# Rotary embedding: the swap of rotated channels by small DMAs and GpSimd in place of permutation matmuls

## The reference

```
h = rms_norm(x, norm_g)
qa, ka, va, za, qb, kb, vb, zb, ga, gb = split(h @ w_in)
qa = partial_rope(qa); ka = partial_rope(ka)       # branch A only; 8 query heads, 2 key heads of 64
ya = swa_sink_attention(qa, ka, va) * silu(za)     # keys: own chunk of 64 and the one before
yb = chunked_relpos_attention(qb, kb, vb) * silu(zb)
merged = sigmoid(ga + bias_a) * (ya @ w_br_a) + sigmoid(gb + bias_b) * (yb @ w_br_b)
out = rms_norm(x + merged @ w_out, final_g)

def partial_rope(t):            # per head: channels 0-7 are x1, 8-15 are x2, 16-63 stay
    return concat(x1 * cos - x2 * sin, x2 * cos + x1 * sin, rest)
```

## Time and profile before

| | us |
|---|---|
| median of 3 runs (lowest to highest) | 3417.24 (3415.64 to 3418.3) |
| the profiled execution, its own time | 3415.78 |
| its span, first to last instruction | 3414.0 |
| PE busy | 3342.3 (98%) |
| DVE, ACT, POOL busy | 1488.9, 1422.8, 1306.6 (44%, 42%, 38%) |

### The profile page before, as it was taken

How to read it: one execution, slowest core, us unless ns; L and a number is a source line. 1 busy time by engine, 2 the same in 40 slices (tenths; PEclk the granted TensorE clock), 3 DMA queues, 4 the chain that set the end, 5 groups by cost and what they waited for, 6 DMA issues and landing times.

```text
span 3414.0 us, 48305 instructions
## 1 busy us (share of the span) xinstructions
PE 3342.3 (98%) x16328; PEld 2498.0 (73%) x16328; DVE 1488.9 (44%) x3097; ACT 1422.8 (42%) x2969; POOL 1306.6 (38%) x1087
## 2 busy tenths in 40 slices
PE   8999999999999999999999999999999999999998
PEld 6667876678766787667876678766787667876676
DVE  4662355513555135551355513555135551355512
ACT  4443444434444344443444434444344443444432
POOL 3334442345423454234542344423454234542244
PEclk9999999999999999999999999999999999999999
DMA  4222431224311242112421124311242112521123
GB/s 156 62 62 87 172 99 50 62 87 167 99 50 62 87 168 99 50 62 87 168 99 52 61 86 168 98 56 61 83 172 94 55 60 84 173 93 56 56 82 116
DMA packets 97782, 319.53 MB, mean 94 GB/s; under 512 B 9984, under 2 KB 26624, under 8 KB 95360
## 3 DMA queue, kind: packets, MB, share of 16 engines
q1 hardware_dynamic: 97536, 316.34, 28.4%
HBM read 299.52 MB, written 16.78 MB: 93 GB/s over the span
## 4 chain that ended last, share of the span: by engine, by line
PE 85%; issue 6%; DVE 5%; POOL 2%; ACT 1%; DMA 0%; DVEq 0%; POOLq 0%; SPq 0%; ACTq 0%
PE acc L909 16%; PE acc L911 14%; PE acc L910 14%; PE ps_o L1004 6%; PE ps_pt L973 5%; PE sc L953 4%; PE sc L909 3%; PE sc L910 3%; PE sc L911 3%; POOL w_lo L755 2%; PE sc L944 2%; PE sc L851 2%; PE sc L852 2%; PE sc L853 2%; PE sc L876 1%
## 5 line engine op out<-in xcount | busy, mean ns | idle before, releaser
L755 POOL TENSOR_TENSOR w_lo<-w_raw,w_hi 128x512 fp32r<-128x512 f32 x928 | 1209.2, 1309 | 2060.0 <-ACT w_hi L1058 2059.3
L909 PE MATMUL acc<-h_hi,w_hi 128*128 128x512 f32 x2432 | 1010.4, 415 | 2.4 <-DVE q L1316 2.4
L911 PE MATMUL acc<-h_hi,w_lo 128*128 128x512 f32 x2432 | 952.7, 392 | 0.0
L910 PE MATMUL acc<-h_lo,w_hi 128*128 128x512 f32 x2432 | 950.4, 391 | 0.0
L1058 ACT ACTIVATE w_hi<-w_raw 128x512 fp32r<-128x512 f32 x928 | 574.2, 624 | 392.9 <-DMA w_raw<-w 116.5
L909 PEld LDWEIGHTS acc<-h_hi,w_hi 128*128 128x128 f32 x2432 | 456.3, 188 | 212.3 <-issue 133.9
L911 PEld LDWEIGHTS acc<-h_hi,w_lo 128*128 128x128 f32 x2432 | 456.4, 188 | 101.5
L910 PEld LDWEIGHTS acc<-h_lo,w_hi 128*128 128x128 f32 x2432 | 458.1, 188 | 75.7
L1146 ACT ACTIVATE probs_b<-sc,negm 128x640 f32<-128x640 f32 x256 | 203.2, 794 | 373.6 <-DVE negm L1263 373.0
L1153 ACT ACTIVATE probs_t<-ps_pt 128x512 f32<-128x512 f32 (+1 forms) x272 | 150.7, 554 | 264.8 <-PE ps_pt L973 264.8
L1288 DVE SCALAR_TENSOR_TENSOR part<-th,sc 128x512 f32<-128x512 f32 x64 | 43.9, 686 | 468.0 <-PE sc L911 467.8
(11 more groups left out here) (140 smaller groups left out, 3923.8 us busy)
## 6 DMA issues: line engine op xcount, KB each, us to landing
w_raw<-w SPq DMA_DIRECT2D x464, 512.0 KB, 3.5
rows<-x SPq DMA_DIRECT2D x36, 512.0 KB, 7.4
xt<-x_t SPq DMA_DIRECT2D x16, 1024.0 KB, 10.0
out<-rows SPq DMA_DIRECT2D x32, 512.0 KB, 2.8
x_in<-x SPq DMA_DIRECT2D x28, 512.0 KB, 5.4
cs<-rope_tab SPq DMA_DIRECT2D x8, 512.0 KB, 4.3
bias<-near SPq DMA_DIRECT2D x1, 1024.0 KB, 13.3
g_out<-final_g SPq DMA_DIRECT2D x1, 512.0 KB, 11.5
```

The lines of the kernel that those rows point to most:

```text
L755: pool.tensor_tensor(w_lo[n % 2][:, c], w_raw[n % 2][:, c], w_hi[n % 2][:, c].bitcast(FP32), ALU.subtract).then_inc(w_split, 1)
L909: pe.matmul(dst[:, :], hi, src_hi[:, k, :], start=begin, stop=False)
L910: pe.matmul(dst[:, :], hi, src_lo[:, k, :], start=False, stop=False)
L911: mm = pe.matmul(dst[:, :], lo, src_hi[:, k, :], start=False, stop=end)
```

## The change

The permutation matmuls, `pre_hi`, `pre_lo` and four DVE operations go. ACT makes only `pre`, in one of two buffers in turn. SP then waits until ACT has emptied the bank and issues four DMAs from SBUF to SBUF, each of 8 channels by 512 tokens, which put the swapped channels into `rot` (also two buffers, zero in the channels that do not turn; the second one shares its place with other data and is set to zero anew in each block). POOL multiplies `pre` by the cosines into the destination (step `rope_in`), and in step `rope` waits for the four DMAs, multiplies `rot` by the signed sines and adds. `rope` of `q1` to `q3` stands one quarter later in the list, and the four score tiles of head pair 0 and their exponentials stand two quarters later.

```diff
-        at_ = QUARTERS * O_TILES + 14 + t
+        at_ = QUARTERS * O_TILES + 16 + t
         lead[at_] = [("scores", 0, t), *lead[at_], ("exps", 0, t)]
...
-            fill[at_ + 2] = [("rope", s), *fill[at_ + 2]]
+            fill[at_ + 3] = [("rope", s), *fill[at_ + 3]]
...
-USES_ACC = ("job", "turn_v", "rope_k", "rope", "norm")
+USES_ACC = ("job", "turn_v", "norm")
...
+            def swap(b, step):
+                i = ROPE_NO[("rope_k" if step[1] == "k" else "rope", step[2])] % 2
+                wait_freed(sp, b, step)
+                for h0 in (0, HD):
+                    for to, src in ((h0, h0 + HALF_ROT), (h0 + HALF_ROT, h0)):
+                        sp.dma_start(rot[i][to:to + HALF_ROT, :], pre[i][src:src + HALF_ROT, :]).then_inc(rope_swapped[i], 16)
...
                     if step[0] == "mm" and step[2] == 0 and not (last and step[1] + 2 >= NW):
                         load_w(b, step[1] + 2)
+                    elif step[0] == "job" and step[1] in ("k", "q") and step[2] < PAIRS:
+                        swap(b, step)
...
+                    if step == ("mm", TILES.index(("k", 0)), 0):
+                        hold(h_done, (b + 1) * KT)
+                        pool.memset(rot[1][:, :], 0.0).then_inc(rot_zeroed, 1)
...
+                        pool.tensor_tensor(roped(step), pre[no % 2][:, :], cs[:, 0, :], ALU.mult).then_inc(rope_cos, 1)
+                    elif step[0] in ("rope", "rope_k"):
+                        no = ROPE_NO[step]
+                        hold(rope_cos, b * NROPE + (no + 1))
+                        pool.wait_ge(rope_swapped[no % 2], b * (64 * (3 - no % 2)) + 64 * (no // 2 + 1))
+                        pool.tensor_tensor(rot[no % 2][:, :], rot[no % 2][:, :], cs[:, 1, :], ALU.mult).then_inc(rope_sin, 1)
+                        pool.wait_ge(rope_sin, b * NROPE + (no + 1))
+                        pool.tensor_tensor(roped(step), roped(step), rot[no % 2][:, :], ALU.add).then_inc(rope_done, 1)
...
-                    elif kind in ("rope", "rope_k"):
-                        claim(b, step)
-                        pe.wait_ge(rope_lo, b * NROPE + (ROPE_NO[step] + 1))
-                        pe.matmul(bank(step)[:, :], perm_r[:, :], pre_hi[:, :], start=True, stop=False)
-                        pe.matmul(bank(step)[:, :], perm_r[:, :], pre_lo[:, :], start=False,
-                                  stop=True).then_inc(acc_full, 1)
...
-                    if not (first and no == 0):
-                        act.wait_ge(rope_done, b * NROPE + no)
-                    act.activation(pre[:, :], ps, ACT.Copy,
+                    if not first or no >= 2:
+                        act.wait_ge(rope_done, b * NROPE + max(no - 1, 0))
+                    if no == 1:
+                        act.wait_ge(rot_zeroed, b + 1)
+                    act.activation(pre[no % 2][:, :], ps, ACT.Copy,
                                    scale=SCALE if name == "q" else 1.0).then_inc(free(step), 1)
-                    wait_freed(act, b, step)
-                    act.activation(pre_hi[:, :], pre[:, :], ACT.Copy).then_inc(rope_hi, 1)
```

More of the change, by code:

```diff
@@ L31 @@
 HD = 64
+HALF_ROT = HD // 8
 PAIRS = 4
@@ L360, with program @@
 check_ring()
-def program(nc, x, x_t, w, near, far, sinks, norm_g, final_g, gate_b, rope_tab, perm, eye, out):
+def program(nc, x, x_t, w, near, far, sinks, norm_g, final_g, gate_b, rope_tab, eye, out):
     off = [(nc.sbuf_base + 63) // 64 * 64]
@@ L408, in program @@
     y_lo_at = y_at + 4 * SETS * BLK
-    pre = at("pre", [P, BLK], FP32, y_lo_at + 4 * BLK * 3)
-    pre_lo = at("pre_lo", [P, BLK], FP32R, y_lo_at + 4 * BLK * 6)
-    pre_hi = at("pre_hi", [P, BLK], FP32R, y_lo_at + 4 * BLK * 7)
+    pre = [at(f"pre{i}", [P, BLK], FP32, y_lo_at + 4 * BLK * n) for i, n in enumerate((3, 6))]
     bias = sb("bias", [P, 9, A_KEYS])
@@ L427, in program @@
     ident = sb("ident", [P, P])
-    perm_raw = sb("perm_raw", [P, P])
-    perm_r = sb("perm_r", [P, P], FP32R)
+    rot = [sb("rot0", [P, BLK]), at("rot1", [P, BLK], FP32, y_lo_at + 4 * BLK * 7)]
     far_sb = sb("far_sb", [P, 8])
@@ L487, in program @@
     pair_valued = sem("pair_valued")
-    rope_hi = sem("rope_hi")
-    rope_lo = sem("rope_lo")
+    rope_swapped = [sem(f"rope_swapped{i}") for i in range(2)]
     rope_cos = sem("rope_cos")
+    rope_sin = sem("rope_sin")
+    rot_zeroed = sem("rot_zeroed")
     rope_done = sem("rope_done")
@@ L519, in program @@
     c_dve = sem("c_dve")
-    N_CONSTS = 6
+    N_CONSTS = 5
     ADDED = HALVES * TT - O_BANKED
@@ L685, in _ @@
             load_w(0, 1)
-            for dst, src in ((perm_raw[:, :], perm), (g_out[:, :], final_g), (bias[:, 0:8, :], near), (far_sb[:, :], far),
+            for dst, src in ((g_out[:, :], final_g), (bias[:, 0:8, :], near), (far_sb[:, :], far),
                              (sink_sb[:, :], sinks), (gb_raw[:, :], gate_b)):
@@ L689, in _ @@
             sp.dma_start(cs[:, :, :], rope_tab[0]).then_inc(cs_in, 16)
+            sp.wait_ge(zeroed, 6)
             def body(b, first, last):
@@ L731, in _ @@
             pool.memset(v_b[:, 0:TT, :], 0.0).then_inc(zeroed, 1)
-            pool.wait_ge(zeroed, 5)
+            pool.memset(rot[0][:, :], 0.0).then_inc(zeroed, 1)
+            pool.wait_ge(zeroed, 6)
             def rsqrt(which, t, n, got, got_count, mid, done, count):
@@ L756, in split_lo, with roped @@
                                    ALU.subtract).then_inc(w_split, 1)
+            def roped(step):
+                return k_a[:, P:P + BLK] if step[0].endswith("_k") else q[POS[step[1]] % 2][:, :]
             rsqrt_x(0)
@@ L782, in body @@
                             pool.tensor_copy(v_b[:, 0:TT, c:c + P], v_b[:, TT:2 * TT, c:c + P]).then_inc(kept, 1)
+                    elif step[0] in ("rope_in", "rope_in_k"):
+                        job_ = ("job", "k" if step[0] == "rope_in_k" else "q", step[1])
+                        bank_, k = WHERE[job_]
+                        hold(acc_free[bank_], b * ON_BANK[bank_] + (k + 1))
+                        if step[0] == "rope_in_k" and not first:
+                            hold(kept, (b - 1) * NKEEP + (KEEP_NO[("keep_k", PAIRS - 1)] + 1))
+                        pool.wait_ge(cs_in, 16 * (b + 1))
+                        no = ROPE_NO[(step[0].replace("_in", ""), step[1])]
+                        pool.tensor_tensor(roped(step), pre[no % 2][:, :], cs[:, 0, :], ALU.mult).then_inc(rope_cos, 1)
[6 more added lines that the diff above has]
+                        pool.tensor_tensor(roped(step), roped(step), rot[no % 2][:, :], ALU.add).then_inc(rope_done, 1)
                     elif step[0] == "next_rstd" and not last:
@@ L826, in _ @@
             turn_rstd(0)
-            pe.wait_ge(zeroed, 5)
+            pe.wait_ge(zeroed, 6)
             def token_products(b, n, c):
@@ L1300, in body @@
                         job_done(b, first, step)
[L1301 to L1319, removed]
                     elif kind == "scores":
@@ L1408, in rope_tables @@
     tab[0] = 1.0
-    perm = np.zeros((P, P), np.float32)
     for h0 in (0, HD):
         for i in range(half):
-            for c in (h0 + i, h0 + half + i):
+            for c, sign in ((h0 + i, -1.0), (h0 + half + i, 1.0)):
                 tab[0, c] = np.cos(ang[:, i])
-                tab[1, c] = np.sin(ang[:, i])
-            perm[h0 + half + i, h0 + i] = -1.0
-            perm[h0 + i, h0 + half + i] = 1.0
+                tab[1, c] = sign * np.sin(ang[:, i])
     tab = tab.reshape(2, P, NBLK, BLK).transpose(2, 1, 0, 3)
-    return np.ascontiguousarray(tab), perm
+    return np.ascontiguousarray(tab)
 def kernel(x, norm_g, w_in, a_sinks, b_rel_bias, w_br_a, w_br_b, gate_bias, w_out, final_g):
@@ L1462 @@
     far = np.ascontiguousarray(np.broadcast_to(b_rel_bias[0][:, 2 * P], (P, 8)))
-    rope_tab, perm = rope_tables()
+    rope_tab = rope_tables()
     arrays = {
@@ L1470 @@
         "gate_b": np.ascontiguousarray(gate_bias[0].reshape(2 * KT, P).T),
[L1471 removed]
+        "rope_tab": rope_tab, "eye": np.eye(P, dtype=np.float32),
     }
```

6 lines of the change are left out of this document (2 added, 4 removed).

## The result

The changed kernel takes 3427.28 us (median of 6 runs, 3422.96 to 3431.79), the kernel before 3416.33 (6 runs, 3415.22 to 3418.3): the ratio is 1.0033, 95% [1.002, 1.0045]. It is slower by some 11 us, where 12.7 us less was forecast, and it lies just outside the range. The profiled execution took 3425.59 us, its span 3423.8.

What follows compares the result with a forecast made beforehand. PE, busy 98% of the span, was taken as the bound. Per block -2.87 - 1.15 + 1.58 + 0.85 = -1.59 us, times 8 is -12.7: 3403.1, with 1.5 for the median 3404.6, rounded 3405; range 3383 to 3426.

Steps and rivals of the forecast that it cites:

- step 5: Loads of tiles 7 and 8 wait behind swap issues on SP, so `turn_v` starts 1.58 us later per block (+0.8 to +5.9).
- rival C: Both loads land after 5.4 us in place of 3.6 behind the small DMAs: 29 us more, 3434; chance 0.05.
- Rival B: PE's 3.2 us wait at `turn_v` drops the clock, eight times 2.5 us on top of the forecast: 3425; chance 0.13.
- points 2 and 3: Per block, removed matmuls of `q1` to `q3` save 2.87 us; PE's waits for DVE's and ACT's rotary work save 1.15.
- point 6: Scores of the first pair two quarters later: PE waits 0.85 us per block for ACT's copy of the first transposes.
- Points 1 and 5: Removed matmuls of `k0` and `q0` save 0.94 us per block, a gain counted inside the later loads' 1.58 us cost.
- rival A: Full gain: the loads do not decide, `turn_v` keeps its 0.69 us wait, -4.11 us per block, 3384; chance 0.17.
- Points 7 and 8: POOL's 15 new operations per block cost nothing; DVE operations meeting POOL taken as nothing, 7.4 us kept for the range.

Runs made afterwards that it cites:

- e3: The changed kernel with 18 matmuls that nobody reads added per block ahead of `turn_v`, to fill PE's wait: 3413.18 us, ratio 0.9988.
- e10: The changed kernel with two swap DMAs in place of four per rotary, the second head of each pair not swapped: 3396.54 us, ratio 0.9944.
- e7: The changed kernel with the swap of `k0` alone issued behind the next tile's load, the query swaps still ahead of theirs: 3399.67 us, ratio 0.9944.
- e1: The changed kernel with SP issuing every swap behind the next tile's load and not ahead of it: 3376.28 us, ratio 0.9878.
- e4a: The kernel before with only the four score tiles of pair 0 and their exponentials two quarters later: 3419.66 us, ratio 1.0011.
- e11: e1 with the four score tiles of pair 0 back at their old place, two quarters earlier: 3371.05 us, ratio 0.9867.
- e8: e1 with POOL making the cosine product of each rotary twice, 40 operations more: 3378.9 us, ratio 0.989.

## Why the prediction was wrong

Two steps failed: step 5, "the loads behind the swaps", put the four issues at 1.80 us where they took 2.82, and the sum put the fall of the clock at nothing, where it cost 16.5 us. It took both to turn the sign. By the sum at the end of this section the kernel would be 4.6 us faster than before without the fall, and e3, which has the late loads without the fall, is 4.4 us faster (3413.18 against 3417.59).

**Step 5, the term that was mis-sized.** The chain was the right one, and all its parts but one agree within 0.1 us: the landing (3.6 and 0.10 forecast, 3.62 together), copy to issue (0.65, 0.62), split to copy (0.53, 0.54). The four issues were taken from loads issued in pairs, 0.45 each, 1.80 us. They took 2.82 us to the load, 0.70 each. Twice 1.02 is 2.04, of which the other parts, slightly shorter, give back 0.2: the chain from copy to `turned` was 15.18 long and not 13.36, and `turn_v` came 3.38 later and not 1.58. In eight blocks that is 14.4 us. The landing of 3.6 also answers rival C, which had 5.4. e10 confirms it: the mean wait goes from 40.1 / 8 = 5.01 to 18.9 / 8 = 2.36, 2.65 less, where two turns save 2 x (2.82 - 1.48) = 2.68. The bounds (0.8 to 5.9) held this, but they were made by a landing of 5.4; the issue was given no more than 0.54, because the rows at hand were all of loads over 128 partitions. The step named the four issues as its weak place, rightly, and the range did not draw on it far enough.

**Rival B came true on top.** With 3.2 us of waiting it had 0.13. The waits were 4.8 to 5.2, and the clock fell in all eight blocks. The price was put at 2.5 us each from the start of the kernel; it is 1.4 to 2.8, 16.5 in all, and e3 shows 14.1 of it by filling the wait. The Trainium skill, "TensorE: Matmul & The Clock Gate", section "What's actually happening", which takes the throttled state as the default and activity as its release, goes with e3: same lateness, PE active, clock at 1.00. Even at the forecast 3.2 us the fall was probably the likelier outcome: no run has a wait of that length, but at 2.2 to 2.9 us, in e7 and e10, it came in 11 of 16 blocks. Against the fall the prediction had only the longest wait seen without one, 1.6 us, which, as it says itself, tells nothing of 3.2. That B's time of 3425 lies near the measured 3427 is in part luck: 14.0 us that B lacks in step 5 stand against 2.6 in points 2 and 3, 3.3 in point 6 and 3.7 in the price of the fall that it has too much.

**Points 1 and 5 together, rival A.** e1 is A made real: `turn_v` keeps its 0.69, and the front takes 17.17 in place of 18.15, 0.98 less (0.94 forecast). A's time was 3384; e1 has 3376, because of the next two points.

**Points 2 and 3.** Forecast 2.87 + 1.15 = 4.02 per block, measured 4.54 in block 3, in after and in e1 alike, and 4.35 in the mean of the eight (3.50 in block 0). The waits for `gate`, `whole` and `q` are gone entirely. Which steps hold what is over 4.02 I have not placed.

**Point 6.** Forecast 0.85 (its own figures give 0.89), measured 0.42, in after, in e4a and in reverse in e11. The mechanism is there in the new row, PE waiting for `probs_t` on ACT, but with 0.3 us a block, 2.2 us in eight times, and not some 0.8; the two exponentials were not so much in the way as thought.

**Points 7 and 8.** POOL at 1459.7 us (1460 forecast). PE waits for nothing of `rot` or of the rotated channels, and the 15 new operations of 1.27 to 1.30 us cost PE little: 5 more per block cost 0.4 us in e8. They do hold up DVE. Its operation `part<-rden`, which took 0.54 us at most before, took up to 1.22 us after (view by tile, ns, min/median/max; before, then after):

```profile
L1354 DVE TENSOR_SCALAR part<-rden x64: 426/427/542, 78.0 to 3240.2; 128x512 f32<-128x512 f32 x64
...
L1364 DVE TENSOR_SCALAR part<-rden x64: 426/427/1217, 84.2 to 3249.6; 128x512 f32<-128x512 f32 x64
```

It is the same place in each of the eight blocks, beside POOL's `rot<-rot,cs` and `q<-q,rot`, and it is an operation with one input tensor, not two. PE does not wait for it, so the 7.4 us kept for this were not needed.

**The sum again, with what was measured**, block by block and added up over the eight: fill -34.8, step 5 +26.7, T0 to T1 +3.5, the two stages with the fall of the clock +16.3. That is +11.7; the profiled executions differ by 3425.59 - 3415.78 = 9.8. The rest, -1.9, lies behind the branch matmuls, where the blocks of one kernel differ by up to 1.5 us among themselves, so I read no effect in it.

## What to carry to other kernels

A DMA's price is also its issue, here 0.7 us each for four small ones: what stands behind it in the same queue waits for the semaphore it waits for and then for every issue, however few bytes they move. Where a prefetch and a transfer that waits for fresh data share a queue, put the prefetch first; that order was worth 51 us here. An edit that comes out 11 us slower can still hold a gain of 41 us, so it should be read stage by stage before it is dropped.

## What was not expected of the hardware

- An issue on SP of a DMA of 8 partitions by 512 (16 KB, SBUF to SBUF) took 0.625 us, the next one started 0.68 later, where a load of 512 KB takes 0.34. The small transfer was the dearer one to issue. The Trainium skill, "DMA: Bandwidth & Descriptors", section "Issuing engines are not separate DMA queues", calls the sequencer's time to initiate a DMA usually small relative to the DMA itself; here the measurement decides otherwise: 0.625 us of issue is not small beside the at most 2.0 us from the start of an issue to its landing, and the four together hold the queue for 2.8. What makes the issue dear was not tested; these DMAs differ from the loads in partitions, in size and in where they read.
- The swaps themselves landed fast: the last issue of the four starts at 1303.22 + 2.68 - 0.62 = 1305.28, and POOL's operation that waited for them started at 1307.31, so 2.0 us at most, less than the 3.6 of a load.
- Waits of like length gave both clock levels: in e10 it fell after 2.18 and held after 2.47, in e7 it fell after 2.66 and held after 2.89. The length of the wait alone does not decide there. At the start of the kernel, some 26 us in, it held after 1.69 us in after and fell after 1.79 in e7 and after 2.14 in e8. After 4.8 to 5.2 us it fell each time, after 1.6 or less never. What else decides was not looked into.
